# Query projection as seven block products instead of eight, in a hybrid attention and mixture-of-experts block

## The reference, cut to what matters

```python
h = rms_norm(x, norm1_g[l])                      # x: 256 tokens x 1024
proj = h @ w_in[l]                               # 1024 x 3652
q, k, v, qi, ki, wi, pool_in, gate_a, gate_p = jnp.split(proj, split_at, axis=-1)
q = rope(rms_norm(q.reshape(b, s, ATTN_HEADS, HEAD_DIM), q_norm_g[l]), positions)   # q: 512 columns
k = rope(rms_norm(k...), positions)
attn = dsa_attention(q, k, v, qi, ki, wi)        # 64 keys chosen per query by an indexer
merged = sigmoid(gate_a) * (attn @ w_branch_attn[l]) + sigmoid(gate_p) * (pooled @ w_branch_pool[l])
x = x + merged @ w_out[l]
x = x + moe_ffn(rms_norm(x, norm2_g[l]), ...)    # top-4 of 32 experts, 1024 wide
```

## Time and profile before

| | |
|---|---|
| median of 3 runs | 1087.96 us (1086.49 to 1088.13) |
| the profiled execution, its own time | 1087.61 us |
| its span, first to last instruction | 1085.5 us |
| what lies around the span | 2.11 us |
| mean granted TensorE clock | 0.986 of 2.4 GHz |
| PE busy | 1048.6 us (97%) |
| DVE busy | 382.1 us (35%) |
| the query projection on PE | 24.58 to 38.32 us from the span's start |

### The profile page before, as it was taken

The page is one execution under the profiler, slowest core; times in us unless marked ns, Lnnn a source line. Parts: engine busy times, 40 slices in busy tenths (PEclk is TensorE's granted clock), DMA queues, the critical chain, the costliest instruction groups (busy, mean ns, idle before and its releaser), DMA issues.

```text
span 1085.5 us, 12191 instructions
## 1 busy us (share of the span) xinstructions
PE 1048.6 (97%) x4830; PEld 424.3 (39%) x4830; DVE 382.1 (35%) x709; ACT 121.8 (11%) x215; POOL 15.3 (1%) x31
## 2 busy tenths in 40 slices
PE   8999999999999999999998999899989999898998
PEld 6445445344343434343432434242424333332432
DVE  3797685123232332232322222222222312232222
ACT  3115213100000001000000000000000000000001
POOL 4000000000000000000000000000000000000000
PEclk9999999999999999999998999899999999999999
DMA  9905796999999999999999999999999999999996
GB/s 328 371 38 194 280 420 259 398 430 414 427 430 429 427 429 435 429 428 432 430 429 431 430 426 430 432 430 435 432 430 429 431 432 430 431 431 424 428 428 263
DMA packets 37065, 430.44 MB, mean 397 GB/s; under 512 B 4225, under 2 KB 6401, under 8 KB 16433
## 3 DMA queue, kind: packets, MB, share of 16 engines
q1 hardware_dynamic: 35328, 427.59, 93.6%
q0 software_dynamic: 1136, 1.91, 0.5%
q10 hardware_dynamic: 576, 0.60, 0.2%
HBM read 429.03 MB, written 1.05 MB: 396 GB/s over the span
## 4 chain that ended last, share of the span: by engine, by line
PE 71%; DMA 27%; DVE 1%; SPq 1%; issue 1%; ACT 0%; ACTq 0%; DVEq 0%
PE bank L1634 29%; DMA ring<-w_gate_up_dram 24%; PE bank L1663 14%; PE bank L1559 5%; PE bank L1372 5%; PE bank L1221 4%; PE bank L1586 4%; DMA ring<-w_down_dram 3%; PE bank L1652 2%; PE bank L1513 2%; PE bank L1247 1%; PE bank L1427 1%; PE bank L1181 1%; PE bank L1612 1%; SPq L317 0%
## 5 line engine op out<-in xcount | busy, mean ns | idle before, releaser
L1634 PE MATMUL bank<-ring,scr 128*64 128x512 f32 x2032 | 475.6, 611 | 27.5 <-DMA ring<-w_gate_up_dram 27.3
L1634 PEld LDWEIGHTS bank<-ring,scr 128*64 128x64 f32 x2032 | 141.1, 140 | 325.5 <-issue 284.5
L1663 PE MATMUL bank<-ring,scr 128*64 128x512 f32 x992 | 225.1, 595 | 0.1
L1121 DVE TENSOR_TENSOR x<-bank,x 128x512 f32<-128x512 f32 x120 | 77.3, 686 | 254.6 <-PE bank L1586 254.6
L1663 PEld LDWEIGHTS bank<-ring,scr 128*64 128x64 f32 x992 | 68.8, 137 | 127.6 <-issue 122.9
L1096 DVE COPY scr<-bank 128x512 f32<-128x512 f32 x32 | 22.1, 692 | 257.9 <-PE bank L1634 257.9
L1102 DVE TENSOR_TENSOR scr<-bank,bgu 128x512 f32<-128x512 f32 x64 | 41.2, 686 | 98.6 <-PE bank L1652 98.6
L1586 PE MATMUL bank<-scr 64*128 64x512 f32 x240 | 67.7, 641 | 0.1
L583 ACT ACTIVATE scr<-bank 128x512 f32<-128x512 f32 x32 | 19.1, 598 | 383.4 <-PE bank L1634 383.4
L1559 PEld LDWEIGHTS bank<-scr,xn 128*128 128x128 f32 x480 | 54.8, 192 | 13.0 <-issue 13.0
L1559 PE MATMUL bank<-scr,xn 128*128 128x128 f32 x480 | 57.8, 278 | 0.0
(11 more groups left out here) (226 smaller groups left out, 527.9 us busy)
## 6 DMA issues: line engine op xcount, KB each, us to landing
ring<-w_gate_up_dram SPq DMA_DIRECT2D x40, 4096.0 KB, 31.5
ring<-w_down_dram SPq DMA_DIRECT2D x62, 2048.0 KB, 17.5
ring<-w_gate_up_dram SPq DMA_DIRECT2D x40, 2048.0 KB, 17.6
ring<-w_gate_up_dram SPq DMA_DIRECT2D x13, 1024.0 KB, 8.8
ring<-w_in_dram SPq DMA_DIRECT2D x12, 1024.0 KB
ring<-w_out_dram SPq DMA_DIRECT2D x4, 1024.0 KB
ring<-w_down_dram SPq DMA_DIRECT2D x4, 1024.0 KB, 29.9
ring<-w_branch_pool_dram SPq DMA_DIRECT2D x2, 1024.0 KB
```

The costliest lines, as they stand in the source:

```text
L1121: V.tensor_tensor(x[:, b, 512 * h:512 * h + 512], XY[h][:, :], x[:, b, 512 * h:512 * h + 512], ALU.add).then_inc(read[f"Y{j}"], 1)
L1634: ins = MM(GB[h][T * g:T * g + T, :], xgT[:, k, T * e:T * e + T], w[:, c0:c0 + 512], start=k == 0, stop=k == KC - 1)
L1663: ins = MM(DB[T * h:T * h + T, :], actT[e][:, c, :], v3(dn_slot[j][:, :], 4)[:, k, 512 * h:512 * h + 512], start=c == 0, stop=c == KC - 1)
```

## The change

The query's 1024 x 512 weights become 2x2 blocks of 512 inputs by 256 columns: `w11`, `w12` are the two column halves of unit 4, `w21`, `w22` those of unit 5. With the sums s1 to s4 that the gates use anyway, seven block products give the same result as eight. Each is 4 products of 256 columns on PE. Four of the seven (a11 w11, s2 t2, s1 t1, s4 w22) accumulate in bank 4, one after another, and ACT copies the bank out after each of them, because each partial sum is a value that some output block needs. Three others (a12 w21, s3 t3, a22 t4) go to banks 5, 3 and 2, and DVE adds them to the copies in four small adds (`query_add`). DVE also makes four differences of weight blocks (`query_part`), 128 x 1024 each. The semaphores of the attention branch's block products are renamed and shared; their counts are shifted. SP's thresholds on `job_ready` are lowered by 2, since the query no longer signals it.

```diff
+        query_w = [v3(half[u], 4)[:, :, 256 * h:256 * h + 256] for u in (4, 5) for h in range(2)]
+        query_t1, query_t2 = v3(siga_t[:, 0:1024], 4), v3(siga_t[:, 1024:2048], 4)
+        query_out = [qq[:, b, 256 * h:256 * h + 256] for b in range(NB) for h in range(2)]
...
             job(0, kvx[:, :, 0:290])
             job(1, kvx[:, :, 290:580])
+            def query(product, i, b, signal, n):
+                act.wait_ge(block_prod, product)
+                nc.scalar.activation(query_out[i], bank[4][:, 0:256], ACT.Copy, scale=small[:, 128 + b:129 + b]).then_inc(signal, n)
+
+            query(1, 0, 0, block_copied, 1)
             root(132, 6, 2)
-            job(2, qq)
+            query(3, 2, 1, block_copied, 1)
+            query(5, 3, 1, block_copied, 1)
+            query(7, 1, 0, job_read, 2)
             root(140, 16, 3)
...
+            def query_part(i):
+
+                w11, w12, w21, w22 = query_w
+                out, a, b = [(query_t1, w12, w11), (w12, w22, w12), (query_t2, w22, query_t1), (w11, w21, query_t2)][i]
+                if i == 0:
+                    dve.wait_ge(unit_in[4], 16)
+                else:
+                    dve.wait_ge(block_part, i)
+                if i == 1:
+                    dve.wait_ge(unit_in[5], 16)
+                elif i == 3:
+                    dve.wait_ge(block_prod, 1)
+                V.tensor_tensor(out, a, b, ALU.subtract).then_inc(block_part, 1)
+
+            def query_add(i, b, acc, product, copied, before):
+
+                dve.wait_ge(block_prod, product)
+                dve.wait_ge(block_copied, copied)
+                if before:
+                    dve.wait_ge(query_added, before)
+                V.scalar_tensor_tensor(out=query_out[i], in0=acc[:, 0:256], scalar=small[:, 128 + b:129 + b], in1=query_out[i],
+                                       op0=ALU.mult, op1=ALU.add).then_inc(query_added, 1)
+
+            for i in range(3):
+                query_part(i)
...
             root_and_reciprocal(132, 6, 1.0 / HD, 2)
+            query_part(3)
             scaled(k4, KV, 132, rows[:, R_KG:R_KG + HD])
...
             part(0, 0)
             part(0, 1)
+            query_add(0, 0, bank[5], 2, 1, 0)
+            query_add(3, 1, bank[3], 5, 3, 0)
+            query_add(2, 1, bank[3], 5, 2, 0)
+            query_add(2, 1, bank[2], 6, 2, 3)
+            dve.wait_ge(query_added, 4)
             dve.wait_ge(job_read, 6)
             head_squares(q4, HEADS, 140)
...
-            for j in range(1, 4):
-                projection(j)
+            projection(1)
+
+            def query_projection():
+
+                w11, t3, w21, w22 = query_w
+                t4 = w11
+
+                def product(acc, lhs, rhs, fresh):
+                    for k in range(4):
+                        ins = MM(acc[:, 0:256], lhs[:, k, :], rhs[:, k, :], start=fresh and k == 0, stop=k == 3,
+                                 skip_group_check=not fresh)
+                    ins.then_inc(block_prod, 1)
+
+                unit(4)
+                product(bank[4], a11, w11, True)
+                unit(5)
+                product(bank[5], a12, w21, True)
+                pe.wait_ge(block_copied, 1)
+                pe.wait_ge(sums_ready, 4)
+                pe.wait_ge(block_part, 3)
+                product(bank[4], s2, query_t2, False)
+                pe.wait_ge(job_read, 4)
+                product(bank[3], s3, t3, True)
+                pe.wait_ge(block_copied, 2)
+                product(bank[4], s1, query_t1, False)
+                pe.wait_ge(block_part, 4)
+                product(bank[2], a22, t4, True)
+                pe.wait_ge(block_copied, 3)
+                product(bank[4], s4, w22, False)
+
+            query_projection()
+            projection(3)
...
                 unit(8 + 4 * g)
                 if g == 0:
-                    pe.wait_ge(job_read, 4)
+                    pe.wait_ge(query_added, 4)
                 else:
                     pe.wait_ge(job_read, 8)
```

More of the change, by code:

```diff
@@ L280, in block_kernel @@
         N_PROD, N_SUM, OUT_PROD = 7, 7, 14
-        LAST_OF_BRANCH = {17: 2 * (BJ_WB + NB)}
-        ATT_PROD = 7
+        LAST_OF_BRANCH = {17: 2 * (BJ_WB + NB - 1)}
+        BLOCK_PROD, BLOCK_PART, BLOCK_COPY = 7, 4, 3
+        ATT_M, ATT_P, ATT_S, ATT_C = 7, 4, 0, 3
         block = ctx.enter_context(nc.Block())
@@ L290, in unit_free @@
                 if u < 8 and u % 2 == 1:
-                    sp.wait_ge(job_ready, u + 1)
+                    sp.wait_ge(job_ready, u + 1 if u < 4 else u - 1)
                 elif u < 8:
@@ L342, in _ @@
             load_gu(4, 1)
-            sp.wait_ge(job_ready, 2 * (BJ_WB + NB))
+            sp.wait_ge(job_ready, 2 * (BJ_WB + NB - 1))
             load_gu(7, 1)
-            sp.wait_ge(att_prod, ATT_PROD)
+            sp.wait_ge(block_prod, ATT_M + BLOCK_PROD)
             load_gu(5, 1)
@@ L553, in copy_att @@
             def copy_att(product, dst):
-                act.wait_ge(att_prod, product)
-                nc.scalar.activation(dst, bank[2][:, :], ACT.Copy).then_inc(att_copied, 1)
+                act.wait_ge(block_prod, ATT_M + product)
+                nc.scalar.activation(dst, bank[2][:, :], ACT.Copy).then_inc(block_copied, 1)
             copy_att(1, att_p1)
@@ L728, in part @@
                     if g == 1:
-                        dve.wait_ge(job_ready, 6)
+                        dve.wait_ge(block_prod, BLOCK_PROD)
                 elif i == 1:
@@ L907, in att_parts @@
                 else:
-                    dve.wait_ge(att_part, i)
+                    dve.wait_ge(block_part, ATT_P + i)
                 if i == 3:
-                    dve.wait_ge(att_prod, 1)
-                V.tensor_tensor(out, a, b, ALU.subtract).then_inc(att_part, 1)
+                    dve.wait_ge(block_prod, ATT_M + 1)
+                V.tensor_tensor(out, a, b, ALU.subtract).then_inc(block_part, 1)
             def att_sums(i):
@@ L921, in att_sums @@
                 else:
-                    dve.wait_ge(att_sum, i)
-                V.tensor_tensor(out, a, b, op).then_inc(att_sum, 1)
+                    dve.wait_ge(block_sum, ATT_S + i)
+                V.tensor_tensor(out, a, b, op).then_inc(block_sum, 1)
             def merge(b, h, branch_out):
@@ L940, in _ @@
             out_part(1)
-            dve.wait_ge(att_copied, 1)
-            dve.wait_ge(att_prod, 2)
+            dve.wait_ge(block_copied, ATT_C + 1)
+            dve.wait_ge(block_prod, ATT_M + 2)
             step(V.tensor_tensor(att_p1, bank[3][:, :], att_p1, ALU.add))
             merge(0, 0, att_p1)
-            dve.wait_ge(att_copied, 2)
-            dve.wait_ge(att_prod, 4)
+            dve.wait_ge(block_copied, ATT_C + 2)
+            dve.wait_ge(block_prod, ATT_M + 4)
             step(V.tensor_tensor(att_u2, bank[4][:, :], att_u2, ALU.add))
-            dve.wait_ge(att_copied, 3)
+            dve.wait_ge(block_copied, ATT_C + 3)
             step(V.tensor_tensor(att_u4, bank[4][:, :], att_u4, ALU.add))
             merge(1, 1, att_u4)
-            dve.wait_ge(att_prod, 7)
+            dve.wait_ge(block_prod, ATT_M + 7)
             merge(0, 1, bank[2][:, :])
@@ L1435, in attention_branch @@
                 product(bank[3], t12, w21, True)
-                pe.wait_ge(att_copied, 1)
-                pe.wait_ge(att_part, 3)
-                pe.wait_ge(att_sum, 4)
+                pe.wait_ge(block_copied, ATT_C + 1)
+                pe.wait_ge(block_part, ATT_P + 3)
+                pe.wait_ge(block_sum, ATT_S + 4)
                 product(bank[2], n2, att_t2, False)
@@ L1441, in attention_branch @@
                 product(bank[4], n3, t3, True)
-                pe.wait_ge(att_copied, 2)
+                pe.wait_ge(block_copied, ATT_C + 2)
                 product(bank[2], n1, att_t1, False)
                 turn_merged(0, 0)
-                pe.wait_ge(att_part, 4)
+                pe.wait_ge(block_part, ATT_P + 4)
                 product(bank[5], t22, w11, True)
-                pe.wait_ge(att_copied, 3)
+                pe.wait_ge(block_copied, ATT_C + 3)
                 product(bank[2], n4, w22, False)
```

8 lines of the change are left out of this document (4 added, 4 removed).

## The result

The changed kernel takes 1089.88 us as the median of 8 runs (1087.87 to 1091.58), the kernel before 1087.53 (1086.24 to 1088.47, 8 runs). The ratio is 1.0024 with a 95% interval of 1.0015 to 1.0033: about 2.6 us slower (1.6 to 3.6); the medians lie 2.35 apart. The forecast was 1089.5. The seven block products save what they should on PE, and the kernel is slower all the same.

The account below looks back on a forecast made before the run. DVE, gapless from 41.06 us, was to hold PE at two places in the attention stage: minus 1.70 us of products plus the waits nets +1.7, passed on by the loop, giving 1089.5 us (range 1087.0 to 1091.9).

Parts of the forecast that it names:

- Products: Query projection on PE: 28 products at 0.43 us take 12.04 in place of 13.74, a gain of 1.70 us.
- No wait inside the query projection: PE in the query projection: transfers, weight differences and bank copies come in time, 0.2 to 0.7 us in hand.
- DVE before 38.44 costs nothing: DVE's added weight differences vanish in its wait for unit 10 until 38.44, 1.1 us left; uncovered, up to 3.4 us.
- the 38.6 that was named as a sign of being wrong: DVE's `part(0, 0)` was to start at 38.44; a start later than 38.6 us would show the forecast wrong.
- The four adds cost 1.86: DVE's gapless stretch after 41.06: adds of 0.49 us each delay the norm by 1.86; bounds 1.6 and 2.1.
- First place: PE's transposes at 55.72, waiting for DVE's `part(0, 2)`: some 3 us of wait, then +1.4 to +1.6 us late.
- second place: PE's transposes at 72.66, waiting for DVE's first `gate_sum`: start at 74.3 to 74.5, +1.63 to +1.85 us.
- The loop passes it on: Expert loop: a shift of PE in the attention stage moves the transfers, the loop and the end one for one.
- rival 2: PE's new wait near 54 to 57 lowers its clock: 2.8 us more, +4.2 in all, 1091.8 us; chance 0.12.
- a clock below 1.00 between 54 and 62: PE's granted clock behind the new wait: below 1.00 from 54 to 62 us would show the forecast wrong.
- the gain stays: Attention stage: DVE does not bind, so PE stays 1.7 us early and the time is 1086.1 us; chance 0.12.
- More waits in the query projection: Query projection: unit 5 lands over 1.1 us later than counted, 0.5 to 1 us more, 1090.2 us; chance 0.08.

Follow-up runs that it names:

- execution c: The changed kernel, nothing edited, profiled once more (third further look); 1091.81 us.
- b: The changed kernel, nothing edited, profiled once more (second further look); 1090.94 us.
- d: The changed kernel, nothing edited, profiled once more (fourth further look); 1090.12 us.
- e2: Changed kernel with adds ahead of `part(0, 0)`, `part(0, 2)` right behind `part(0, 1)`, first two gate sums earlier; 1086.38 us, 0.9992 of before.
- e3: Changed kernel without its four adds, so the query is incomplete; 1087.00 us, 1.0001 of the kernel before.
- e1: Changed kernel with its four adds moved ahead of `part(0, 0)`, into DVE's wait for DMA; 1087.24 us, 1.0000 of the kernel before.
- e9: The kernel with adds, third part and gate sums all moved earlier, timed again unchanged on another chip; 1086.58 us, 0.9992 of the kernel before.
- e6: Changed kernel with adds and `part(0, 2)` moved earlier but the gate sums at their old place; 1087.91 us, 1.0012 of the kernel before.
- e7: Changed kernel with a second set of four adds, results unused, behind the first; 1092.94 us, 1.0048 of the kernel before.
- e4: The kernel before, eight products, plus four extra adds with unused results behind `part(0, 1)`; 1089.17 us, 1.0016 of the kernel before.

## Why the prediction was right, and where it was short

By its own steps, with the profile after beside them:

1. **Products.** 28 at 0.43 were to take 12.04 us; they took 12.09. The gain was to be 1.70 and was 1.65. The projection began 0.14 us later than before (24.72, against 24.58), which no step had.
2. **No wait inside the query projection.** Right: one piece of 56 records. Unit 5 landed at 24.76 (24.8 to 25.3 was worked out). In execution c, where PE was 0.6 us early, it waited 0.26 us, which costs nothing, as the wait at the first place is that much shorter.
3. **DVE before 38.44 costs nothing.** Right: 1.28 us of wait left, 1.1 foreseen. (`part(0, 0)` started at 38.41, but at 38.62, 38.70 and 38.89 in b, d and c, past the 38.6 that was named as a sign of being wrong; there the late transfer adds its tenths.)
4. **The four adds cost 1.86.** They took 1.88, and the norm started 1.91 behind the first. One add took 0.48 (0.474 to 0.483), which is the 0.49 taken from L798 and not the 0.42 of the lower bound.
5. **First place +1.4 to +1.6, second +1.63 to +1.85, net +1.7.** Measured +1.45, +1.71, and +1.77 at the loop. The handover behind `part(0, 2)` was 0.10 us, and the second wait some 0.24, where 0.2 to 0.5 was forecast.
6. **The loop passes it on.** Gauge and ratio agree to within 1 us, the width of one interval to either side, in all nine timings: +4.74 gave +5.2 us, +2.03 gave +1.7, +1.77 (the change) gave +2.6, +1.20 gave +1.3, -1.37 gave -0.9. That the loop takes a delay up is refuted. For a lead it is open: PE in e2 has lost its 1.36 us by 544, and still the span is 1.0 us shorter.

The size is where it was short. The sum gives +1.7; the ratio says +2.6, and 1.6 to 3.6 with its interval, so that +1.7 lies just inside. That the 1089.5 came within 0.4 us of 1089.88 is in part luck: it was counted from 1087.96, a median of three, and the median of eight is 1087.53. The step that was mis-sized is the one between forecast and rival 2: "the wait lets the clock fall" got 0.12 as a thing that would happen or not, and "a clock below 1.00 between 54 and 62" was named as a sign of being wrong. It happens in some executions and not in others. Two of five profiled ones had it, and by their mean clock six of the eight timed ones probably did, which was not seen in a trace for these. The rows shown had two waits, 2.11 us without and 4.15 us with the earlier trace rows, and the wait that was worked out, some 3 us, lies between. But the same trace has six more in the expert loop, of 2.53 to 4.15 us, and behind every one of them the 16 records took 4.99 to 6.02 us in place of 3.65:

```profile
753.00 5.35 PE L1634 MATMUL bank<-ring,scr 128*64 128x512 f32 x16 [2.53 <-DMA ring<-w_gate_up_dram]
...
811.43 5.35 PE L1634 MATMUL bank<-ring,scr 128*64 128x512 f32 x16 [3.20 <-DMA ring<-w_gate_up_dram]
```

(From 754 to 757 and from 812 to 815 us the granted clock is 0.50.) Of the seven waits over 2.5 us all were followed by the lower clock, which speaks for far more than 0.12. At the first place it stayed with 2.76 to 2.87 us in three of three and fell with 3.29, 3.36 and 4.51 in three of three. The length does not settle it: in the loops of the runs, waits of 2.35 to 2.53 us were followed by the lower clock, and those of 2.28 to 2.32 were not, while 2.87 at the first place was not either. So the right forecast had two cases with a mixed median: +1.8 to +2.0 where the clock stays, and +3.1 and +4.8 as b and c show. The rival's price of 2.8 us is that of c; b paid 1.4. The Trainium skill, "TensorE: Matmul & The Clock Gate", in its part on the HAM clock gate, says that the monitor does not start afresh with a kernel, so that the point of a change varies from run to run; the five executions agree that it varies, though here the wait varied as well and the two causes were not told apart.

The other rivals: *the gain stays* is refuted by e3, where it is gone even without adds. *More waits in the query projection* came true in c, in e1 (0.33 us, unit 5 at 25.07) and in e9 (0.31 us, unit 5 at 25.70). In the changed kernel they cost nothing, as that step said; in e9, where the adds stand ahead of `part(0, 0)` and nothing covers a late landing, the lateness of unit 5 went through to the loop.

Open is the spread of e6: its times of 1087.03 to 1090.97 have two groups, and only one execution was profiled. Its wait at the second place, 2.21 us, was followed by full clock there; whether longer ones in the slower group were not is not known.

## What to carry to other kernels

Saved work on the busiest engine is worth only the margin that the engine beside it has where the two meet; read that margin (0.53 and 0.27 us here) first, and count what the saving adds to the other engine at full price. Where the two meet twice, both places have to be freed, as e6 and e2 show. And before a new wait is taken for harmless, look at what followed every wait of about its length in the trace at hand, not at two of them; the length alone did not decide here, so forecast both cases, for the same kernel may show both. The loop here, which waits for its transfers, passed a delay of PE on to the end; that it passes on a lead as well is likely from the times and not shown on PE.

## What the runs showed of the hardware

- At one place, a PE wait of 2.87 us was followed by full clock, one of 3.29 us by a clock of 0.72 from 58 to 62 us, one of 3.36 us by 0.50, in executions of one and the same program. In the loop a wait of 2.53 us, behind products at full clock, was followed by 0.50 from 754 to 757 us.
- The loss from a fallen clock did not follow the length of the wait: estimated from the windows, 1.4 us in b, 2.9 in c, 1.5 in e7, although e7 had the longest wait, 4.51 us. It followed how much work PE did before the clock was back.
- The same transfer lands at times up to 1.1 us apart (unit 5 from 24.61 in e2 to 25.70 us in e9, one and the same program; from 24.76 to 25.16 in the five executions of the changed kernel), read from the start of the DVE instruction that waits for it.
- The four adds, three of them free of each other and one behind, took 1.88 to 1.89 us in every kernel that had them in the query; the four with unused results took 1.78 in e4 and 1.79 in e7.
